# A hybrid decoder layer on one core: finer pieces and a new combine order at the end, the last low part on VectorE, and the split residual stored in the residual's own order

## What is computed

```python
h = rms_norm(x, norm_mix_w)
q, k, v, z, b, a, rx, rgate = split(h @ w_in)
y = concat(gated_deltanet_group(q, k, v, z, b, a), rglru_group(rx, rgate))   # 8 + 8 groups of 128 channels
x = x + y @ w_out
h = rms_norm(x, norm_ffn_w)
# router: softmax over 4 groups, the best group, in it the best 2 of 8 experts
for e in range(32):                                # all 32 experts, top 2 of them per token
    he = silu(h @ w1[e]) * (h @ w3[e])             # 2048 -> 512
    moe += combine[:, e:e+1] * (he @ w2[e])        # 512 -> 2048
return rms_norm(x + moe, norm_final_w)
```

## Time and profile before

| | |
|---|---|
| time, median of 3 (range) | 1462.45 us (1461.41 to 1463.6) |
| profiled execution: time / span | 1461.75 us / 1459.6 us |
| busy: TensorE / VectorE / ScalarE / GpSimd | 92% / 43% / 30% / 5% |
| HBM read | 478.96 MB, 330 GB/s over the span |
| mean granted TensorE clock | 0.983 |

### The profile page before, as it was taken

The page is one execution under the profiler, slowest core; times in us unless marked ns, Lnnn a source line. Parts: engine busy times, 40 slices in busy tenths (PEclk is TensorE's granted clock), DMA queues, the critical chain, the costliest instruction groups (busy, mean ns, idle before and its releaser), DMA issues.

```text
span 1459.6 us, 20147 instructions
## 1 busy us (share of the span) xinstructions
PE 1339.3 (92%) x7702; PEld 831.2 (57%) x7702; DVE 627.3 (43%) x1112; ACT 442.5 (30%) x849; POOL 66.6 (5%) x64
## 2 busy tenths in 40 slices
PE   4999999999999898898898899899889799889986
PEld 3899999999988743443353343343343344335332
DVE  5968888888865611231222212222213123222323
ACT  5455656656654411111021011110111111102112
POOL 0012220122100000000000000000000000000000
PEclk9999999999999999999999999999999999999998
DMA  7665555455546869999999999999999999999995
GB/s 200 155 154 154 153 149 153 128 155 149 197 142 214 356 268 429 426 427 429 427 428 429 428 428 429 429 425 423 428 427 427 427 429 427 428 430 428 427 425 215
DMA packets 147648, 481.75 MB, mean 330 GB/s; under 512 B 11450, under 2 KB 113043, under 8 KB 122131
## 3 DMA queue, kind: packets, MB, share of 16 engines
q1 hardware_dynamic: 147602, 481.10, 84.0%
HBM read 478.96 MB, written 2.12 MB: 330 GB/s over the span
## 4 chain that ended last, share of the span: by engine, by line
PE 64%; DMA 26%; DVE 6%; ACT 2%; issue 1%; SPq 1%; DVEq 0%; ACTq 0%
PE bank L601 63%; DMA ew<-in_expert_w_dram 23%; DMA mixT<-in_expert_w_dram 3%; PE bank L604 1%; DVE w_parts L1503 1%; DMA fw<-in_norm_ffn_w_dram 0%; SPq L545 0%; ACT fw_r L1339 0%; DVE hT L2006 0%; DVE ew L1542 0%; DVE ew L2029 0%; DVE fw L1463 0%; ACT ew L1414 0%; DVE fw L2072 0%; SPq L481 0%
## 5 line engine op out<-in xcount | busy, mean ns | idle before, releaser
L601 PE MATMUL bank<-ew,hT 128*64 128x512 f32 (+1 forms) x1556 | 465.4, 603 | 63.0 <-DMA ew<-in_expert_w_dram 38.1
L601 PEld LDWEIGHTS bank<-ew,hT 128*64 128x64 f32 (+1 forms) x1556 | 156.4, 142 | 357.5 <-issue 357.2
L601 PE MATMUL bank<-act_parts,w_parts 128*128 128x256 f32 x2304 | 308.9, 288 | 1.7 <-DVE w_parts L1503 1.7
L601 PEld LDWEIGHTS bank<-act_parts,w_parts 128*128 128x128 f32 x2304 | 285.9, 192 | 3.3 <-issue 1.4
L601 PE MATMUL bank<-ew 128*64 128x512 f32 (+2 forms) x1120 | 249.9, 577 | 6.8 <-DVE ew L2031 6.8
L601 PE MATMUL bank<-mixT,hT 128*64 128x512 f32 x512 | 232.3, 608 | 0.0
L2017 DVE TENSOR_TENSOR fw<-fw,bank 128x512 f32<-128x512 f32 x128 | 79.1, 680 | 230.0 <-PE bank L601 230.0
L601 PEld LDWEIGHTS bank<-ew 128*64 128x64 f32 (+1 forms) x1120 | 85.2, 142 | 148.9 <-issue 133.1
L1412 ACT ACTIVATE ew<-bank,gs 128x512 f32<-128x512 f32 x32 | 22.0, 687 | 481.0 <-PE bank L601 481.0
L1503 DVE TENSOR_TENSOR w_parts<-fw,w_parts 128x2048 fp32r<-128x2048 f32 x64 | 147.7, 2312 | 25.7 <-ACT w_parts L1104 24.7
L1432 ACT ACTIVATE ye_r<-bank 64x512 fp32r<-64x512 f32 x128 | 75.7, 591 | 203.7 <-PE bank L601 202.1
(11 more groups left out here) (245 smaller groups left out, 1080.1 us busy)
## 6 DMA issues: line engine op xcount, KB each, us to landing
ew<-in_expert_w_dram SPq DMA_DIRECT2D x157, 2048.0 KB, 17.1
mixT<-in_expert_w_dram SPq DMA_DIRECT2D x32, 2048.0 KB, 19.8
fw<-in_w_in_dram SPq DMA_DIRECT2D x48, 1024.0 KB, 5.9
fw<-in_w_out_dram SPq DMA_DIRECT2D x16, 1024.0 KB, 5.0
ew<-in_expert_w_dram SPq DMA_DIRECT2D x4, 1024.0 KB, 18.0
mixT<-in_x_dram SPq DMA_DIRECT2D x1, 2048.0 KB, 7.5
fw<-in_x_dram SPq DMA_DIRECT2D x1, 2048.0 KB, 9.7
out_dram<-fw SPq DMA_DIRECT2D x4, 512.0 KB, 2.7
```

What stands on the lines that cost most here:

```text
L601: return nc.tensor.matmul(o, l, r, start=start, stop=stop, skip_group_check=True)
```

## The change

Three parts:

- **Layout of the split residual.** `high_rows` and `low_rows` now read and write contiguously, in the order of `x2`. The step of 16 elements moves into the gather: the weight load of every gather matmul now reads `hn_hi` or `hn_lo` with a step of 64 bytes (128 elements per load).
- **Last low part.** The quarter that GpSimd made is made by VectorE, between its last routing instruction and its wait for `s_rank`. The fillers before the rank matmuls go from 12 to 16, those after from 14 to 8.
- **End.** The last expert's pieces 0, 1 and 5 come in halves too. Four of the eight combine blocks begin with a matmul of the identity with `x2` (`residual`), placed where TensorE waits for `hs` and `g` and after the down matmuls. Combine takes the first 512 columns of each Y half first, and starts when only these are split. ScalarE copies the four blocks that hold the residual into `x2`, VectorE adds the other four. ScalarE's square root table is loaded earlier. The last 1024 columns are scaled and stored in two blocks of 512.

```diff
+LAST = ((0, 0), (0, 2), (1, 0), (1, 2), (0, 1), (0, 3), (1, 1), (1, 3))
+LAST_BANK = (6, 7, 0, 1, 2, 3, 4, 5)
+HELD = 4
+STORES = tuple((t, slice(a, b)) for t, a, b in ((0, 0, 1024), (0, 1024, 2048), (1, 0, 1024), (1, 1024, 1536), (1, 1536, 2048)))
...
+                for half in range(2):
+                    for c, landed in ((slice(0, D), s_ew), (slice(D, 2 * D), s_ewl)):
+                        for piece in (2 * half, 2 * half + 1):
+                            sp.wait_ge(s_ed, (r * NE + NE - 2) * 6 + piece + 1)
+                            sp.dma_start(ewp[piece][:, c], expert_piece(NE - 1, piece)[:, c]).then_inc(landed[piece], 16)
...
-            keep_going(12)
+            keep_going(16)
...
-            keep_going(14)
+            keep_going(8)
...
-                            l = mm(o[:, c * T:(c + 1) * T], (hn_lo if lo else hn_hi)[t][:, k * P:(k + 1) * P],
+                            rows = (hn_lo if lo else hn_hi)[t].rearrange("q (p k) -> q k p", k=KD)[:, k, :]
+                            l = mm(o[:, c * T:(c + 1) * T], rows,
...
+            def residual(n, i):
+
+                t, col = LAST[i]
+                for tile in range(NT):
+                    pe.wait_ge(s_add[tile], n * 8 + 4)
+                mm(bank[LAST_BANK[i]][:, :], ident, x2[:, t, col * 512:(col + 1) * 512], True, False)
+
+            def combine_last(n, ends):
+
+                m = pe.snap(n * 2 + 1)
+                pe.wait_ge(s_yeA, m * 8 + 6)
+                pe.wait_ge(s_yl, ends)
+                for i, (t, col) in enumerate(LAST):
+                    if i == 4:
+                        pe.wait_ge(s_yeA, m * 8 + 8)
+                        pe.wait_ge(s_yeD, m * 2 + 2)
+                    o = bank[LAST_BANK[i]][:, :]
+                    w = placeT[:, 1, col // 2, t * P:(t + 1) * P]
+                    c = slice(col % 2 * 512, col % 2 * 512 + 512)
+                    mm(o, w, y_hi[:, col // 2, c], i >= HELD, False)
+                    mm(o, w, y_lo[col // 2][:, c], False, True).then_inc(s_comb, 1)
...
-                act.activation(hn_hi[t].rearrange("q (k p) -> q k p", k=KD)[:, :, lo:hi],
-                               x2[:, t].rearrange("q (p k) -> q k p", k=KD)[:, :, lo:hi], ACT.Copy).then_inc(s_hnH, 1)
+                act.activation(hn_hi[t][:, lo * KD:hi * KD], x2[:, t, lo * KD:hi * KD], ACT.Copy).then_inc(s_hnH, 1)
...
+                for i in range(HELD):
+                    t, col = LAST[i]
+                    act.wait_ge(s_comb, m * 8 + i + 1)
+                    act.activation(x2[:, t, col * 512:(col + 1) * 512], bank[LAST_BANK[i]][:, :], ACT.Copy)\
+                        .then_inc(s_add[t], 1)
...
+            dve.wait_ge(s_hnH, 4)
+            low_rows(1, 96, P)
             dve.wait_ge(s_rank, 1)
...
-                adds(dve.snap(r * NQUAD + (NQUAD - 1)), 1)
...
+                for i in range(HELD, 2 * 4):
...
-            pool.wait_ge(s_hnH, 4)
-            G.tensor_tensor(hn_lo[1].rearrange("q (k p) -> q k p", k=KD)[:, :, 96:P],
-                            x2[:, 1].rearrange("q (p k) -> q k p", k=KD)[:, :, 96:P],
-                            hn_hi[1].rearrange("q (k p) -> q k p", k=KD)[:, :, 96:P], ALU.subtract).then_inc(s_hnL, 1)
```

More of the change, by code:

```diff
@@ L433, in build @@
         s_ahead = sem("s_ahead")
-        s_ewl = [sem("s_ewl0"), sem("s_ewl1")]
+        s_ewl = [sem(f"s_ewl{b}") for b in range(4)]
+        s_ewk = sem("s_ewk")
+        s_yl = sem("s_yl")
         s_pick = sem("s_pick")
@@ L1011, in quad @@
                         for k in range(KD // 2):
-                            if last and j == QUAD - 1 and half == 1 and k == KD // 4:
+                            if last and j == QUAD - 1 and k == KD // 4:
                                 for which in range(2):
-                                    pe.wait_ge(s_ewl[which], ends * 16)
+                                    pe.wait_ge(s_ewl[half * 2 + which], ends * 16)
                             if j == 0 and k % 2 == 0:
@@ L1029, in quad @@
                         gates_next(pe.snap(n + 1))
+                    final = last and j == QUAD - 1
+                    if final:
+                        residual(n, 0)
                     pe.wait_ge(s_hs, e + 1)
@@ L1041, in quad @@
                         gather_next(pe.snap(n + 1))
+                    if final:
+                        for i in range(1, HELD - 1):
+                            residual(n, i)
                     pe.wait_ge(s_g, e + 1)
@@ L1051, in quad @@
                         w2 = ewp[4 + which].rearrange("p (k n) -> p k n", n=D)
+                        if final and which == 1:
+                            for k in (2, 3):
+                                if k == 3:
+                                    pe.wait_ge(s_ewk, ends * 16)
+                                for i in range(2):
+                                    for side in range(2):
+                                        col = (side ^ (j % 2)) * HD2 + i * 512
+                                        l = mm(bank[4 + i][side * 64:side * 64 + 64, :], gT[:, k, :],
+                                               w2[:, k - 2, col:col + 512], False, k == 3)
+                                    if k == 3 and i == 0:
+                                        l.then_inc(s_Y, 1)
+                            l.then_inc(s_ed, 1)
+                            residual(n, HELD - 1)
+                            continue
                         for i in range(2):
@@ L1070, in _ @@
                 quad(pe.snap(r * NQUAD + (NQUAD - 1)), NQUAD - 1, False, True, ends=pe.snap(r + 1))
-                for t in range(NT):
-                    combine(pe.snap(r * NQUAD + (NQUAD - 1)), 1, t)
+                combine_last(pe.snap(r * NQUAD + (NQUAD - 1)), pe.snap(r + 1))
         @block.scalar
@@ L1415, in quad @@
                                    ACT.Tanh, scale=0.5).then_inc(s_eth, 1)
+                    if last and j == QUAD - 1:
+                        act.activation(stat[:, 6:7], eps_c[:, 0:1], ACT.Sqrt)
                     if j == 1:
@@ L2050, in quad @@
                                                 ALU.subtract)
+                        if last and j == QUAD - 1 and i == 0:
+                            l.then_inc(s_yl, 1)
                     l.then_inc(s_yeD, 1)
@@ L2069, in _ @@
                 link(V.reciprocal(stat[:, 4 + t:5 + t], stat[:, 2 + t:3 + t]))
[L2070 to L2073 removed]
+                for tile, c in STORES:
+                    if tile == t:
+                        V.scalar_tensor_tensor(x2[:, t, c], x2[:, t, c], stat[:, 4 + t:5 + t], wfin[:, c],
+                                               ALU.mult, ALU.mult).then_inc(s_fin, 1)
         @block.gpsimd
```

40 lines of the change are left out of this document (18 added, 22 removed).

## The result

The changed kernel took 1491.57 us (median of 4 runs, 1487.05 to 1497.08) beside 1462.52 us for the kernel before (4 runs). The ratio is 1.0202, 95% interval 1.0187 to 1.0218: slower by 29 us. The forecast was 1458.4 and its range ended at 1473.

What follows compares the result with a forecast made beforehand. The weight stream was taken to bound the experts, TensorE only freeing buffers in time. 0.5 + 0.65 - 0.3 + 1.65 + 0.25 + 0.55 = 3.3 us off 1461.75 gave 1458.4 us; range over the cases 1456.6 to 1473.

Steps and rivals of the forecast that it cites:

- The gather with strided weight loads: Gather on TensorE: strided loads keep the 0.12 us spacing of `hs` and cost nothing; forecast's chance 0.45.
- The second rival: Gather: strided weight loads take 0.224 us each, as ScalarE's strided copy suggests; time 1472.2 us, chance 0.31.
- The second rival's price for the later gathers: Seven later gathers: issue gap of 19.5 us plus 2 us exceeds the stream by 1 to 2 us each, about 7 us.
- four pieces of 4.9 us, 19.6 us of stream, are still to come: Later gathers: between issues 14.1 us apart, this much stream remains, so some 4 us more can be hidden.
- The second rival's first gather: First quad's gather, on the path: loads of 0.224 us cost 6.8 us.
- Router: Before the first gather: copies 0.3, cast 0.53, less 0.2 for VectorE and 0.15 for fillers; 0.5 us earlier in all.
- the cast's 0.53 us: Router: without GpSimd's subtraction, the index cast of 698 ns takes 170 ns, saving 0.53 us.
- The fillers' charge of 0.15 us: Before the first gather: 8 fillers let half speed reach further into it, charged 0.15 us, with 1.7 us as other bound.
- End, pieces, residual matmuls and clock: Last experts: halved pieces gain 0.65 us, residual matmuls cost 0.3, full clock in the last down matmuls gains 1.65.
- The third rival: Half speed in the first gather or last down matmuls takes back about 1.6 us each; 1460.0 us, chance 0.12.
- End, order: Combine after the last down matmuls: the new order starts the second square sum earlier, gaining 0.25 us.
- End, last store: End of the kernel: last store of 256 KB in place of 512 KB gains 0.6 us, less 0.06 for an instruction.

Runs made afterwards that it cites:

- run 6: Changed kernel, but the gather's weight loads read 128 neighbouring values, so it picks other columns and computes something else; 1462.45 us.
- run 4: Changed kernel with the split residual stored in runs of four, so the gather's weight loads have a step of 16 bytes; 1502.45 us.
- run 5: Changed kernel with the split residual stored in runs of two, so the gather's weight loads have a step of 8 bytes; 1462.78 us.
- run 3: Changed kernel with `hn_hi` in the old order and `hn_lo` in the new, so every second gather weight load is strided; 1474.35 us.
- run 7: Changed kernel with only the first quad's gather strided by 64 bytes, the seven later gathers loading neighbouring values; 1467.66 us.
- run 1: Kernel before with only the layout of the split residual changed; 1496.92 us, ratio 1.0228.
- run 2: Changed kernel with the old layout (strided copies, contiguous weight loads), all else of the change kept; 1463.19 us, ratio 1.0008.
- run 10: Kernel before with the router's part alone: last low part on VectorE, 16 and 8 fillers, old layout; 1463.65 us, ratio 1.0002.
- run 11: Changed kernel with old layout, last low part behind the third seat mask, TensorE's wait for it after loading `nrounds`, 28 and 22 fillers; 1459.67 us.
- run 9: Kernel before with the change's end alone, plus bf16 matmuls that nothing reads ahead of three TensorE waits; 1460.78 us, ratio 0.9992.
- run 12: Kernel of run 11 plus extra bf16 matmuls that nothing reads ahead of three TensorE waits; 1459.76 us, ratio 0.9984.

## Why the prediction was wrong

**The gather with strided weight loads: wrong, and the step that decides.** The prediction took the spacing of `hs`, 0.12 us, because it is a row of the same engine and instruction, and so put the strided loads at nothing. The changed kernel measured 0.223 us from load to load, and this term is the loss: 1491.57 us with it, 1462.45 without it (run 6). These gathers had no spare time (7.82 of 8.90 us), and run 4 shows that even the step of `hs` costs the full price here. The prediction had noted that the loads "have no spare time" and gave that less weight than the row of `hs`. ScalarE's copy, 1.75 ns per element, gave the right number at 0.224 us. What the two have in common is a memory access with one value for each 16 bytes (runs 4 and 5). Why the loads of `hs` take only 211 ns, with the same step of 16 bytes, is not shown. The second rival stood at 0.31 with the right mechanism.

**The second rival's price for the later gathers: too small by a factor of three to four.** It said 1 to 2 us each and took the lower end, 7 us in all; the traces give 27.5 us, the medians 23.9. That is why even this rival, at 1472.2, and the range with it ended 19 us below the measured time. (Its figure for a spacing of 0.25 us is also added up wrong: 8.4 us for the first gather and seven times 3 us on 1458.4 give 1488, not 1482.) The step "four pieces of 4.9 us, 19.6 us of stream, are still to come" treats the queue as full up to a limit and the loss as over once the next piece is on its way. Over the runs, the price of a later gather (D to L above 862.2, divided by 7) is 1.2 us at a gap of 16.3 us (run 3: D to L 870.7), 3.9 at 19.7 (after) and 5.0 at 20.4 (run 4: 897.6). The price begins below the bound of the prediction, which with its 2 us allows a gap of 17.6. The stream also falters twice behind a gather that ends at 636.8, after 2 us and again 13 us later (the clock column is 1.00, the DMA share 0.06 and 0.60; before, the share was 1.01 over the whole 860 us):

```profile
639.00:641.00 2.00, 2.00 (x12) 0.67 (x10) 0.00 (x0) 0.00 (x0) 0.00 (x0) 1.00 0.06 25
652.00:653.00 1.00, 1.00 (x6) 0.29 (x4) 0.00 (x0) 0.00 (x0) 0.00 (x0) 1.00 0.60 147
```

And TensorE's "75 us of slack over 860" are hardly slack for this: TensorE does 5.4 us more in a quad and gets back only 1.5. I read it so: the buffers hold one expert, and a gather's delay has to be made up within that expert or it is lost. No run changed the buffers, so this reason is not tested.

**The second rival's first gather: about right.** It said 6.8 us; t0 to D gives 6.0, with the router's 0.4 already off it, and the medians of runs 6 and 7 give 5.2.

**Router: the durations right, one cause doubtful, the sum wrong.** The copies (1.6 and 1.7 forecast, 1.49 and 1.76 measured) and the casts (all near 170 ns) are as foreseen. The first gather starts at 508.16 in place of 508.68, 0.5 us earlier where 0.65 was forecast: 0.1 us at t0, and 0.4 us behind it (9.38 us after t0 before, 8.98 in the changed kernel). But the move of the low part to VectorE is not what brought it. The layout alone (run 1) has it too, with the gather 8.88 us after t0, though GpSimd still subtracts:

```profile
501.35 1.26 POOL L2104 TENSOR_TENSOR fw_r<-fw,fw_r 128x512 fp32r<-128x512 f32 x1 [66.74 <-ACT fw_r L1340]
...
502.63 0.29 DVE L1877 CAST misc<-i8u 128x8 f32<-128x8 uint32 x2
```

GpSimd is done at 502.61 there, just before these two casts start, and no cast is slow. And with the low part on VectorE but the old layout (runs 2 and 10) the gather starts 9.35 and 9.31 us after t0, hardly earlier than before. So the cast's 0.53 us was a right number, and contiguous copies were enough to save it; what the move adds is not seen.

The fillers' charge of 0.15 us was mis-sized. With 8 fillers TensorE idles 1.9 us ahead of the gather and half speed falls into it: 5.18 us in place of 4.04 in runs 2 (5.19), 6 and 10. The router term was +0.5 and measured -0.8 (run 6, t0 to D). With the low part late and 22 fillers the loss is gone (run 11, 3.66 us). The other bound, 1.7 us, was the nearer one to the 1.14 lost.

**End, pieces, residual matmuls and clock: 2.0 forecast, 1.1 to 1.2 found.** The last expert starts without a wait for DMA and its down matmuls run in 7.09 us, as foreseen. But L to T went only from 45.27 to 44.1, because half speed moved to expert 30's second up half, 1.6 us. Run 10 shows the old end at 43.94 when half speed falls there. Where no group lost clock (run 9) the new end takes 43.58; the old end less the 1.70 us of its last down matmuls would be 43.57. So pieces and residual matmuls together are worth nothing that these traces show, against 0.35 forecast. The residual matmuls cost what was charged: from the end of the last up half to the first down matmul it is 2.9 us before (1431.63 to 1434.54) and 3.2 us after (1465.33 to 1468.54). The pieces are the mis-sized part: where expert 30 kept the full clock, the last expert waited 0.88 us for its second halves (run 9) in place of 1.13 us before it started, so 0.25 us and not 0.65. The 1.65 us of clock are paid or not by where half speed falls. The third rival named two places, the first gather and the last down matmuls, and missed two others.

**End, order: 0.25 forecast, 0.1 found.** Square sums start at T+5.3 and T+7.5, within 0.1 us of the forecast.

**End, last store: 0.55 forecast, nothing found.** T to end is 16.15 to 16.25 with five stores, 16.26 and 16.27 with four (the layout alone, with combine at half speed, left aside). The last scaling ends 3.1 us before the end of the span, with 256 KB in the last store, and ended 3.2 us before it with 512 KB. From the second tile's scaling on the stores are one stream: the DMA share is 0.86 from 1485.9 to the end of the changed kernel, and in the second fence 0.83 over the same part before:

```profile
1485.90:1491.80 5.90, 0.00 (x0) 0.00 (x0) 2.79 (x5) 0.00 (x0) 0.00 (x0) 0.53 0.86 340
```

```profile
1454.00:1459.60 5.60, 0.00 (x0) 0.00 (x0) 2.41 (x2) 0.00 (x0) 0.00 (x0) 0.50 0.83 336
```

So what is left behind the last scaling seems to be stores that queue, and not the last one alone. This was read from two traces and not tried by itself.

**What stays open.** Which of the waits is followed by half speed in a given execution: the same waits of 1.38 and 2.70 us had it in some kernels and not in others. In the profiled executions of runs 9 and 12 the matmuls behind the covered waits ran at full clock, but the medians moved by 0.95 us and by nothing. And why the gather's delay is not made up later in a quad has a reading here and no test.

## What to carry to other kernels

A matmul chain whose weight loads are already busy for nearly 90% of the time (7.82 of 8.90 us) has no room for a step of 16 bytes or more. Before laying a tile out anew, look at who reads it most: here eight copies of 1 to 3 us gained 0.4 us on the path, and 512 loads lost 0.085 us each (5.4 us in 64). If both sides must be served, try two float32 values together in each 16 bytes (in run 5 that cost 8 ns per load and 0.06 us per copy).

Do not spend the slack of a whole stage on a delay that comes at one place of each round: 1.5 of 5.4 us were made up here. And a gain of 1 to 2 us from keeping the clock high in one place is worth forecasting only together with the other waits on the path, where the loss may turn up instead.

## What the runs showed of the hardware

- A float32 weight load of 128x128 in the gather: 188 ns contiguous, 196 with a step of 8 bytes, 332 at 16 bytes, 317 at 64 bytes. From load to load 0.118, about 0.12, 0.234 and 0.223 us. 16 bytes is a little worse than 64.
- ScalarE, 1536 float32 columns: 2.86 us with one value per 16 bytes, 1.55 with two, 1.49 contiguous.
- A group of 32 matmuls of 512 columns takes 7.09 us at full clock and 8.5 to 8.8 us, once 10.0, where the low level is granted in it. Behind the same wait of 2.7 us it took 7.09 in the kernel before and 8.78 in the changed one.
- Two index casts on VectorE took 0.77 us beside a subtraction on GpSimd with a step of 64 bytes (1.51 us long), and 0.29 us where that subtraction was contiguous (1.26 us) and had just ended.
